# Four of twelve expert weight loads per pair move from SyncE's queue to GpSimd's software queue

## The reference: what is computed

```python
def clamped_swiglu(u):
    glu, lin = u[..., ::2], u[..., 1::2]
    glu = jnp.minimum(glu, SWIGLU_LIMIT)
    lin = jnp.clip(lin, -SWIGLU_LIMIT, SWIGLU_LIMIT)
    return glu * jax.nn.sigmoid(SWIGLU_ALPHA * glu) * (lin + 1.0)

def expert(acc, e):                      # 32 experts, one after the other
    wu, bu, wd, bd, cw = e               # wu (1024, 2048), wd (1024, 1024)
    y = clamped_swiglu(t @ wu + bu) @ wd + bd
    return acc + cw[:, None].astype(t.dtype) * y, None
```

## Time and profile before

| | |
|---|---|
| median of three runs | 1280.28 us |
| the profiled execution | 1280.38 us, its span 1278.7 us |
| TensorE busy | 1161.6 us, 91% |
| VectorE, ScalarE, GpSimd busy | 27%, 14%, 5% |
| SyncE's queue q1 | 444.16 MB, 83.7% of 16 engines |
| GpSimd's queue q0 | 13.08 MB, 3.0% of 16 engines |
| the granted TensorE clock, whole span | 0.969, and 1.00 in the expert loop |

### The profile page before, as it was taken

One profiled execution on the slowest core, in us unless ns is written; L12 is line 12 of the kernel. 1 busy time (PEld: TensorE's weight loads), 2 busy tenths in 40 slices (PEclk: granted clock), 3 DMA queues, 4 the chain that ended last, 5 costly groups with the idle time before them and its releaser, 6 DMA issues.

```text
span 1278.7 us, 14238 instructions
## 1 busy us (share of the span) xinstructions
PE 1161.6 (91%) x5525; PEld 478.1 (37%) x5525; DVE 346.4 (27%) x709; ACT 176.3 (14%) x318; POOL 63.1 (5%) x95
## 2 busy tenths in 40 slices
PE   6799994699999999898989899999999898989896
PEld 2687752565333233232323232323232332323232
DVE  1435347023132212222122222222212122121224
ACT  2141151013011011101010100101010101010102
POOL 2300000100000000000000000000000000000000
PEclk9899996797999999999999999999999999999998
DMA  9961199331999999999999999999999999999991
GB/s 365 323 229 66 71 353 323 144 137 60 380 427 425 427 427 428 425 428 427 427 427 427 426 425 428 425 428 427 427 425 427 426 428 427 427 427 427 426 409 50
DMA packets 46092, 461.46 MB, mean 361 GB/s; under 512 B 6925, under 2 KB 8133, under 8 KB 18244
## 3 DMA queue, kind: packets, MB, share of 16 engines
q1 hardware_dynamic: 38850, 444.16, 83.7%
q0 software_dynamic: 6000, 13.08, 3.0%
q10 hardware_dynamic: 1220, 3.92, 0.8%
HBM read 460.77 MB, written 5.74 MB: 365 GB/s over the span
## 4 chain that ended last, share of the span: by engine, by line
PE 65%; DMA 29%; DVE 3%; ACT 1%; issue 1%; POOL 0%; SPq 0%; ACTq 0%; DVEq 0%
PE bank L1410 32%; DMA ring<-in_w_up 25%; PE bank L1300 6%; PE bank L1403 5%; PE bank L890 3%; PE bank L789 3%; PE bank L1431 2%; PE bank L867 2%; PE bank L1213 2%; DMA arena<-in_w_down 2%; DMA ring<-in_w_ada 2%; PE bank L969 1%; PE bank L813 1%; PE bank L953 1%; PE bank L1306 1%; DMA arena<-in_w_router 1%
## 5 line engine op out<-in xcount | busy, mean ns | idle before, releaser
L1410 PE MATMUL bank<-ring,arena 128*64 128x512 f32 x1536 | 364.5, 604 | 19.0 <-DMA ring<-in_w_up 17.2
L1410 PEld LDWEIGHTS bank<-ring,arena 128*64 128x64 f32 x1536 | 96.9, 137 | 263.3 <-issue 212.1
L1431 PE MATMUL bank<-arena 128*64 128x512 f32 x512 | 116.1, 596 | 18.6 <-DMA arena<-in_w_down 18.6
L1431 PE MATMUL bank<-ring,arena 128*64 128x512 f32 x512 | 116.3, 596 | 0.4
L1410 PE MATMUL bank<-arena 128*64 128x512 f32 x512 | 116.1, 595 | 0.0
L1908 DVE TENSOR_SCALAR arena<-bank 128x256 f32<-128x256 f32 x64 | 24.2, 420 | 292.3 <-PE bank L1410 292.3
L1300 PE MATMUL bank<-arena,mods 128*128 128x512 f32 (+2 forms) x204 | 94.4, 629 | 0.0
L753 ACT ACTIVATE arena<-arena 128x512 f32<-128x512 f32 x32 | 20.2, 630 | 504.2 <-DVE arena L1908 504.2
L1898 DVE TENSOR_TENSOR x<-x,bank 128x512 f32<-128x512 f32 x64 | 44.0, 688 | 149.2 <-PE bank L1300 149.2
L1431 PEld LDWEIGHTS bank<-arena 128*64 128x64 f32 x512 | 37.0, 136 | 97.0 <-issue 70.8
L1925 DVE COPY arena<-bank 64x512 f32<-64x512 f32 x32 | 22.0, 688 | 184.8 <-PE bank L1431 184.8
(11 more groups left out here) (315 smaller groups left out, 848.4 us busy)
## 6 DMA issues: line engine op xcount, KB each, us to landing
ring<-in_w_up SPq DMA_DIRECT2D x96, 2048.0 KB, 24.8
arena<-in_w_up SPq DMA_DIRECT2D x32, 2048.0 KB, 25.4
ring<-in_w_down SPq DMA_DIRECT2D x32, 2048.0 KB, 22.9
arena<-in_w_down SPq DMA_DIRECT2D x32, 2048.0 KB, 24.4
ring<-in_w_ada SPq DMA_DIRECT2D x24, 1024.0 KB, 11.6
ring<-in_w_in SPq DMA_DIRECT2D x5, 2048.0 KB, 15.8
arena<-in_state_hgrn POOLq DMA_DIRECT2D x8, 256.0 KB, 8.2
ring<-in_w_out SPq DMA_DIRECT2D x8, 256.0 KB, 11.3
```

The source lines that it names most:

```text
L1410: mm = pe.matmul(B[2 * e + c % 2][64 * a:64 * a + 64, :], lhsT=xTe[:, k, 64 * e:64 * e + 64], rhs=big(n)[:, CH * r + 512 * c:CH * r + 512 ...
L1431: mm = pe.matmul(B[4 + e][64 * a:64 * a + 64, :], lhsT=gT[e].rearrange("p (j a t) -> p j a t", j=4, a=2)[:, k % 4, k // 4, :], rhs=big(n). ...
```

## The change

The four w_down loads of each pair (c8 to c11) are taken out of SyncE's list and put into GpSimd's, with the same condition for room. c8 and c9 stand in front of the gather, c10 and c11 behind it, and the bias load comes last. The w_up loads stay on SyncE. Each w_down chunk gets a semaphore of its own (`down_full`), and the counts that TensorE waits for are changed to match.

```diff
+        down_full = [sem(f"down_full{n}") for n in range(2 * DOWNS)]
...
         def big_landed(engine, c, it):
 
-            engine.wait_ge(big_full[c % BIGS], it * (16 * PER // BIGS) + 16 * (c // BIGS + 1))
+            if c >= 2 * UPS:
+                engine.wait_ge(down_full[c - 2 * UPS], it * 16 + 16)
+            elif c % BIGS < 2 * UPS - BIGS:
+                engine.wait_ge(big_full[c % BIGS], it * 32 + 16 * (c // BIGS + 1))
+            else:
+                engine.wait_ge(big_full[c % BIGS], it * 16 + 16)
...
             def expert_chunk(c, pair):
-                if c < 2 * UPS:
-                    sp.dma_start(big(c), w_up[pair * (2 * UPS) + c]).then_inc(big_full[c % BIGS], 16)
-                else:
-                    sp.dma_start(big(c).rearrange("p (a n) -> p a n", a=2 // DOWNS),
-                                 w_down[pair * (2 * DOWNS) + (c - 2 * UPS)]).then_inc(big_full[c % BIGS], 16)
+                sp.dma_start(big(c), w_up[pair * (2 * UPS) + c]).then_inc(big_full[c % BIGS], 16)
...
-                for c in range(BIGS, PER):
+                for c in range(BIGS, 2 * UPS):
...
             with pool.Fori(0, total) as it:
-                pool.wait_ge(sem("idx_ready"), it + 1)
-                gather_rows()
+                for c in range(2 * UPS, PER):
+                    pool.wait_ge(chunks_used, it * PER + (PRE + c - BIGS + 1))
+                    pool.dma_start(big(c).rearrange("p (a n) -> p a n", a=2 // DOWNS),
+                                   w_down[(it % PAIRS) * (2 * DOWNS) + (c - 2 * UPS)]).then_inc(down_full[c - 2 * UPS], 16)
+                    if c == 2 * UPS + 1:
+                        pool.wait_ge(sem("idx_ready"), it + 1)
+                        gather_rows()
                 pool.wait_ge(chunks_used, it * PER + (PRE + 2 * UPS))
                 up_bias((it + 1) % PAIRS)
```

## The result

The kernel after takes 1289.71 us (six runs, 1287.55 to 1294.64) against 1279.91 (six runs, 1279.34 to 1280.71): a ratio of 1.0082, with an interval of 1.0061 to 1.0104. It is slower, by 10 us; 1288 was forecast. The runs also spread over 7 us where those of before spread over 1.4. The profiled execution took 1290.11 us, span 1288.4, which is 9.7 more than the span of before. What follows is read from these two spans.

A forecast was written before the change was run, and what follows sets the result against it. Early pairs were taken as bound by TensorE, later ones by the DMA engines at 60.0 us a pair. Terms 0 + 0 + 0 + 7.4 and a few tenths for c10 gave 1280.4 + 7.6 = 1288 us, range 1277 to 1305.

The forecast's parts named there:

- Issue work: GpSimd's four added load issues, 2.3 to 4.2 us a pair, are hidden by its idle time: 0.
- Packets: w_down's 16 KB rows on GpSimd's queue: mixing the queues costs and gives nothing, the loop stays at 60.0 us a pair.
- rival of dearer packets: Rival: w_down packets on the software queue cost 5% more, 1.0 us a pair, giving 1303 us; chance 0.15.
- In turn, one packet each: Each DMA engine alternates between the two queues by packet; while both have work a chunk takes 9.9 us.
- hand-worked pair: One steady loop pair worked: c6 and c7 share with c8 and c9 until 19.8 us; waits at c11.
- Software chunks first: Rival: engines serve a w_down chunk's eight rows before returning to SyncE's queue, giving 1322 us; chance 0.07.
- The steady pair: Late loop pairs stay at 60 us with neither queue starved; small waits gather at c7 and c11: 0.
- c10 behind the row numbers, 0 to 1: On GpSimd c10 is issued 3.6 us later than possible, behind row-number wait and gather; c9 hides it: 0 to 1.
- The end of the line: Last pair: TensorE, held until c7 lands, ends 11.0 us after the last landing instead of 3.65: +7.4 us.
- no effect: Rival: the last pair finds c7 early, so the end term is 0 to 2, giving 1281 us; chance 0.18.
- better fed: Rival: two queues feed the DMA engines better, 434 GB/s throughout, -15 + 7.4, so 1273 us; chance 0.10.

The follow-up runs named there:

- ScalarE's queue: Changed kernel with the four w_down loads on ScalarE's hardware queue instead of GpSimd's, gather alone on the software queue: 1287.94 us, ratio 1.0063 against the kernel before.
- four-pair run: w_down on ScalarE's hardware queue, but the last four pairs on SyncE's queue in order of use: 1279.73 us, 0.9993 against the kernel before.
- two-pair: w_down on ScalarE's hardware queue, but the last two pairs on SyncE's queue in order of use: 1280.5 us, 0.9999 against the kernel before.

## Why the prediction was right

Point by point, by its own steps.

- *Issue work, 0*: GpSimd is busy 3.79 us of a pair and was 1.62. No wait of TensorE traces to it.
- *Packets, 0*: right. Where both queues are full the rate is 427 GB/s (727:791), and a second hardware queue gives the same loss as the software queue within what a comparison tells (1287.94 and 1289.71 us). The rival of dearer packets, which wanted 15 us more, falls with that run.
- *In turn, one packet each*: right, though the counts of the earlier trace rows alone did not decide it: they are about ten and eight or nine packets an engine, which could also be one long turn for each queue. The trace after does: chunk against chunk, each queue served 14 packets in 747.5:748.5 already, one us after c8's first rows, and 69 and 66 in 747.5:752.5. A chunk that starts on the second queue lands in 14 us and not in 24, and the chunks that it passes are late by as much as the hand-worked pair says. *Software chunks first* would have landed them near 7.
- *The steady pair*: right in the mean from the fourth pair on, 60.2 us (before 60.3), and in the two places of the waits. The time was right too: worked out were 19.8 us from c8's issue to c7's landing, and 743.6 to 763.2 are 19.6, though by one engine's last rows and not by an even sharing to the end. Wrong in its evenness: a pair is not 60 but 55.3 to 58.5 or 61.8 to 64.2, mostly in turn. After a long pair SyncE's queue has run far ahead and is nearly empty when c8 is issued, and then the DMA engines are short of work for a while. After, in 808:826:

```profile
DMA packets 595, 6.88 MB, mean 382 GB/s; under 512 B 121, under 2 KB 121, under 8 KB 193
q0 software_dynamic: 515, 5.85, 84.0%
q1 hardware_dynamic: 80, 1.03, 13.5%
```

  This step was put at 0. What such stretches cost at the end is not shown: the last landing came 2.2 us later in the trace after, but 0.3 earlier than before with ScalarE's queue (whose rate in 420:1240 is also down, 424 GB/s), and no later in the four-pair run.
- *c10 behind the row numbers, 0 to 1*: the issue did come in the same round as the gather's (755.27, then 756.32), and taking it away (ScalarE's queue) changed nothing that a comparison tells.
- *The end of the line, +7.4*: measured +7.6, from two errors that cancel in part. From c7's landing to the last landing there were 11.6 us and not 9.9 (c9 landed behind c7 and not with it); from c7's landing to the end TensorE took 22.8 and not 20.9, of which 1.65 is the slow clock behind the 2.40 us wait (3.48 and 2.04 in place of the 1.94 and 1.93 us of the same work).

The runs correct this step in one thing: the lag is not made in the last pair. The step tells of a TensorE held by c7 there, and it was (2.40 us), but 8.0 of the 9.7 us were there before that pair began. With ScalarE's queue the last pair had no wait for c7 or any other chunk and the loss was there all the same; loading that pair in order gave back nothing that is clear (1286.97 for 1287.94), and it took two pairs in order to work the lag off. That a sum of +7.4 met +7.6 so closely is also luck: the six executions after spread over 7 us, and only one of them was traced. Of the other rivals, no effect and better fed did not occur: the loss is clear of its interval, and the loop as a whole ran at 423 GB/s, under the 427 of before.

## What to carry to other kernels

When one consumer takes loads in a fixed order through a few buffers, a second queue gives no bandwidth if the DMA engines are already full; it only lets late loads overtake early ones, and the consumer then stands with finished loads behind the missing one. Count what the consumer still has to do when the last load lands: here that grew from one chunk to three, and this was most of the price (7.6 of 9.7 us). If loads are split over queues for another reason, put them back on one queue for the last few rounds: two rounds were enough here, one was not.

## What the runs showed of the hardware

A wait of a few us on TensorE has a price beyond itself. Around the end of the wait of 4.32 us the granted clock was 0.55 (783:788, mostly the level of 1.2 GHz), and the 16 matmuls behind it took 6.12 us in place of 3.60; behind the wait of 2.40 us (1247.51) they were slow too, and behind one of 2.96 us (724.09) they were not. Before, with waits of up to 1.24 us in a late pair, the clock stayed at 1.00 through the loop. Over the whole span TensorE is busy 1175.1 us where it was 1161.6, for the same matmuls. Early in the loop this was worked off (the two-pair and four-pair runs end as before); in the last pair after it cost 1.65 us.

The 16 DMA engines do not finish together. Before, at the end of the loads, in 1246:1250 and then 1250:1254:

```profile
DMA packets 54, 0.46 MB, mean 115 GB/s; under 512 B 26, under 2 KB 26, under 8 KB 26
```

```profile
DMA packets 10, 0.11 MB, mean 29 GB/s; under 512 B 3, under 2 KB 3, under 8 KB 3
```

The second is seven 16 KB packets in 4 us, one after the other at some 0.6 us each: the pace of a single engine, since a sixteenth of 427 GB/s moves 16 KB in 0.61 us. So from about 1250 on one engine is left, and this straggler makes the last landing at 1256.9. Which engine that is, and whether it does more work or runs slower, the records do not say; it stays open.
